# TensorE multiplies constant tiles while it waits: one kernel, 625 extra calls

## What is computed

```python
# first block, two layers, with 256 context tokens beside the 1024
h = rms_norm(x, gain) * (1 + scale) + shift
aq, ak, av, ag, bz, bg, nq, nk, nv, ng = split(h @ w_in)
a = softmax(rope(norm(aq)) @ [rope(norm(ak)), ak_ctx].T) @ [av, av_ctx]     # 8 heads, 2 key heads
b = pooled(bz) @ pool_w                                                     # four window widths
n = softmax([q @ k_neighbours.T + rpb, q @ k_ctx.T]) @ v                    # 4 heads, 8 x 16 window
x = x + gate * (concat(a * silu(ag), b * silu(bg), n * silu(ng)) @ w_out)
# second block
z = rmsnorm(x) @ w_in_2
y_fox = softmax(causal(q @ k.T * scale + c_i - c_j)) @ v                    # 8 heads, forgetting
y_rwkv = scan(r, w, k, v, a, b)             # state by chunks of 64 tokens, 16 chunks, 8 heads
x = x + (gates * (y_fox @ w_o_fox, y_rwkv @ w_o_rwkv)) @ w_out_2
x = x + (gelu(conv(rmsnorm(x) @ w_up)) * conv(...)) @ w_down
x = x + sigmoid(rmsnorm(x) @ w_ple_gate) * (p @ w_ple_up)
```

## Time and profile before

| | before |
|---|---|
| time, median of 3 runs | 4059.61 us (4057.88 to 4069.99) |
| the profiled execution: its time | 4062.47 us |
| its span, first to last instruction | 4060.7 us |
| TensorE busy with matmuls | 3622.6 us, 89% of the span |
| VectorE, GpSimd, ScalarE busy | 47%, 40%, 27% |
| mean granted clock of TensorE | 0.937 |

### The profile page before, as it was taken

One profiled execution on the slowest core, in us unless ns is written; L12 is line 12 of the kernel. 1 busy time (PEld: TensorE's weight loads), 2 busy tenths in 40 slices (PEclk: granted clock), 3 DMA queues, 4 the chain that ended last, 5 costly groups with the idle time before them and its releaser, 6 DMA issues. The chain is left out here.

```text
span 4060.7 us, 58584 instructions
## 1 busy us (share of the span) xinstructions
PE 3622.6 (89%) x25164; PEld 2712.6 (67%) x25164; DVE 1922.8 (47%) x1914; ACT 1098.3 (27%) x1544; POOL 1641.4 (40%) x897
## 2 busy tenths in 40 slices
PE   5999799879899798977999997787888899999988
PEld 4887333668678333766776776764467688888877
DVE  4442566552542565633549204434543562635542
ACT  3223344430223344411245212223410210101120
POOL 1332366442333366443347444402443344444433
PEclk9999799989899799988999999977889899999999
DMA  4012100044111100041211210020032111111111
GB/s 179 32 46 70 52 1 0 15 157 155 58 36 69 26 1 1 15 150 57 90 56 47 98 66 4 4 94 0 1 107 100 42 46 49 52 47 47 52 47 68
DMA packets 93736, 226.85 MB, mean 56 GB/s; under 512 B 28320, under 2 KB 37536, under 8 KB 92592
## 3 DMA queue, kind: packets, MB, share of 16 engines
q1 hardware_dynamic: 76096, 188.75, 13.5%
q10 hardware_dynamic: 17392, 34.48, 2.6%
HBM read 184.36 MB, written 38.83 MB: 55 GB/s over the span
## 5 line engine op out<-in xcount | busy, mean ns | idle before, releaser
L1719 PE MATMUL acc<-h_hi,weights_hi 128*128 128x512 f32 (+1 forms) x928 | 365.9, 394 | 24.6 <-DVE h_lo L1877 18.7
L988 DVE TENSOR_REDUCE part_max<-aux 128x2 f32<-128x856 f32 (+5 forms) x234 | 237.8, 1016 | 224.8 <-PE aux L836 154.8
L1721 PE MATMUL acc<-h_hi,weights_lo 128*128 128x512 f32 (+1 forms) x928 | 340.2, 367 | 0.0
L1720 PE MATMUL acc<-h_lo,weights_hi 128*128 128x512 f32 (+1 forms) x928 | 340.0, 366 | 0.0
L2396 PE MATMUL acc<-h_hi,weights_hi 128*128 128x512 f32 x672 | 274.2, 408 | 25.6 <-DVE h_lo L2674 15.7
L3297 PE MATMUL acc<-h_hi,weights_hi 128*128 128x512 f32 x704 | 276.0, 392 | 12.7 <-DVE h_lo L540 9.2
L3345 POOL TENSOR_TENSOR weights_hi<-weights,ones 128x1024 fp32r<-128x1024 f32 (+1 forms) x66 | 122.5, 1857 | 392.8 <-PE acc L3299 392.8
L3298 PE MATMUL acc<-h_lo,weights_hi 128*128 128x512 f32 x704 | 275.7, 392 | 0.0
L3299 PE MATMUL acc<-h_hi,weights_lo 128*128 128x512 f32 x704 | 275.4, 391 | 0.0
L1891 DVE RECIPROCAL arena<-arena 128x512 f32<-128x512 f32 (+1 forms) x48 | 141.7, 2953 | 263.3 <-ACT arena L1854 263.3
L2398 PE MATMUL acc<-h_hi,weights_lo 128*128 128x512 f32 x672 | 263.5, 392 | 0.0
(11 more groups left out here) (460 smaller groups left out, 8435.9 us busy)
## 6 DMA issues: line engine op xcount, KB each, us to landing
weights<-in_w_in SPq DMA_DIRECT2D x44, 512.0 KB, 3.3
weights<-in_w_up SPq DMA_DIRECT2D x43, 512.0 KB, 3.2
arena<-in_w_mod SPq DMA_DIRECT2D x6, 2048.0 KB, 9.6
weights<-in_w_out SPq DMA_DIRECT2D x21, 512.0 KB, 5.3
weights<-in_w_mod SPq DMA_DIRECT2D x4, 2048.0 KB, 26.4
mixer_gates<-arena SPq DMA_DIRECT2D x32, 256.0 KB, 2.0
x_between<-arena ACTq DMA_DIRECT2D x16, 512.0 KB, 3.8
weights<-in_w_gates SPq DMA_DIRECT2D x16, 512.0 KB, 3.3
```

Source lines behind the costliest of these rows:

```text
L988: nc.vector.tensor_reduce(part_max[:, b % 2, j, :, i:i + 1], max_tile(m)[:, :, 0:cw], AX_X, ALU.max, negate=True).then_inc(max_done, 1)
L1719: nc.tensor.matmul(out, w_hi[:, b, k, :], hi[:, k, cols], start=(k == 0), stop=False)
L1720: nc.tensor.matmul(out, w_hi[:, b, k, :], lo[:, k, cols], start=False, stop=False)
L1721: return nc.tensor.matmul(out, w_lo[:, b, k, :], hi[:, k, cols], start=False, stop=(k == KD - 1))
```

## The change

A function multiplies a constant 128 x 128 float32 tile (`cn["mean"]`, filled with 1/1024) by itself a given number of times, into 128 columns of a PSUM bank whose content nobody needs at that time. It signals nothing. It is called on TensorE ahead of waits. Where a wait guards the bank that is written, that wait is now made ahead of the call (`acc_free`, `kept`, `raw_ready` or `x_added`, and `row_copied` with `max_done` at a new pair). Nothing is removed. The counts, added up over the whole program, are about 625 calls.

```diff
+def keep_busy(pg, bank, times):
+    for _ in range(times):
+        pg.nc.tensor.matmul(bank[:, 0:P], pg.mean[:], pg.mean[:], start=True, stop=True)
@@ multiply
     if maker:
         maker.tensor(pe)
+        keep_busy(pg, acc[:, 0], 36)
         pe.wait_ge(w.parted, 4)
         pe.wait_ge(acc_free, 2)
         for k in range(nk):
+            if k == 2:
+                keep_busy(pg, pg.aux[:, 0], 12)
             maker.ready(pe, k)
...
         if b == 0:
+            keep_busy(pg, acc[:, 0], 16)
             pe.wait_ge(w.half_parted, 1)
...
         mm.then_inc(acc_ready, 1)
+    pe.wait_ge(acc_free, 3)
+    keep_busy(pg, acc[:, 0], 8)
@@ gemm_residual, ahead of the means (10 also in feed_forward)
                 if squares:
+                    if not beside:
+                        keep_busy(pg, pg.aux[:, 1], 10)
                     pe.wait_ge(sq_added, n - 1)
@@ pair_attention
+    n_ahead = len(order)
...
+                    if m == first_piece[b] and p and blocks[b - 1][2] < p:
+                        pe.wait_ge(row_copied, b)
+                        pe.wait_ge(max_done, m)
+                        keep_busy(pg, pg.aux[:, 0], 8 if own_keys else 4)
...
-                for kind, j, *i in order:
+                for at, (kind, j, *i) in enumerate(order):
                     if kind == "max":
+                        if at < n_ahead:
+                            keep_busy(pg, outs[1], first_idle if j == 0 else 2 if pieces[j][0] == 0 else 4)
                         maximum(j)
                     elif kind == "row":
+                        if at < n_ahead:
+                            keep_busy(pg, outs[1], 5)
                         row(j)
@@ transposes of values; neighbourhood attention
+                    if g == 2:
+                        keep_busy(pg, pg.acc[:, 0], 20)
...
+                    if i == 1:
+                        keep_busy(pg, banks[0], 8)
@@ project (44 in branches, 22 in feed_forward, 18 in gemm_gated_residual)
+                    keep_busy(pg, pg.acc[:, 0], 12 if opened else 36)
                     pe.wait_ge(parted, 2)
...
+                        pe.wait_ge(kept, kept_before(j, c))
                         if c == 0:
+                            if j == 2:
+                                keep_busy(pg, pg.acc[:, 0], 8)
                             pe.wait_ge(parted, j + 1)
-                        pe.wait_ge(kept, kept_before(j, c))
@@ rwkv_scan, outer(t, ci, s)
+                    if t >= n_tiles - 2 and s != 1 and (n, s) > (2 * (n_tiles - 2), 2):
+                        keep_busy(pg, region[0], 3)
```

More of the change, by code:

```diff
@@ L254, in part_weights, with multiply @@
             nc.gpsimd.tensor_tensor(w.lo[:, b], w.raw[:, b], full(w.hi[:, b]), ALU.subtract).then_inc(w.parted, 1)
-def multiply(nc, pe, w, rhs, acc, chunks, nk, acc_ready, acc_free, n, turns=1, maker=None, beside=None):
+def multiply(pg, pe, w, rhs, acc, chunks, nk, acc_ready, acc_free, n, turns=1, maker=None, beside=None):
+    nc = pg.nc
     def product(b, c0, cn, kr):
@@ L340, in _ @@
             def _(pe):
-                multiply(nc, pe, w, rhs, pg.acc, chunks, nk, acc_ready, acc_free, n)
+                multiply(pg, pe, w, rhs, pg.acc, chunks, nk, acc_ready, acc_free, n)
             @block.gpsimd
@@ L401, in _ @@
             def _(pe):
-                multiply(nc, pe, w, rhs, pg.acc, chunks, nk, acc_ready, acc_free, n, maker=maker, beside=beside)
+                multiply(pg, pe, w, rhs, pg.acc, chunks, nk, acc_ready, acc_free, n, maker=maker, beside=beside)
                 if squares:
+                    if not beside:
+                        keep_busy(pg, pg.aux[:, 1], 10)
                     pe.wait_ge(sq_added, n - 1)
@@ L683, in __init__, with pair_attention @@
         self.q, self.k, self.keys, self.maxima, self.blocks, self.v, self.bias = q, k, keys, maxima, blocks, v, bias
-def pair_attention(pg, cn, pairs, q_cols, totals, ring, beside=None, mask=None, parts=None):
+def pair_attention(pg, cn, pairs, q_cols, totals, ring, first_idle, beside=None, mask=None, parts=None):
     nc = pg.nc
@@ L2040, in query_pair @@
                         keys=(k_twice[:, kv, :], k_rest[:, kv, :]))
-        pair_attention(pg, cn, [query_pair(p) for p in range(4)], SEQ + q_ctx * P, [by_head(5), total[:]], 4, by_head(4))
+        pair_attention(pg, cn, [query_pair(p) for p in range(4)], SEQ + q_ctx * P, [by_head(5), total[:]], 4, 12 if last else 4, by_head(4))
     pg.end_section()
@@ L2115, in _ @@
                 maker.tensor(pe)
+                keep_busy(pg, pg.acc[:, 0], 18)
                 pe.wait_ge(p_parted, 2)
@@ L2205, in _ @@
             def _(pe):
-                multiply(nc, pe, w, y, pg.acc, MAIN, nk, acc_ready, acc_free, 2 * KD, turns=2)
+                multiply(pg, pe, w, y, pg.acc, MAIN, nk, acc_ready, acc_free, 2 * KD, turns=2)
             @block.gpsimd
@@ L2268, in forgetting_attention @@
         pair_attention(pg, cn, [forgetting_pair(p) for p in range(FOX_TILES)], SEQ,
-                       [k[:, 0, :].rearrange("p (h n) -> p h n", h=2), total[:]], 3, mask=causal[:, 1, :], parts=parts)
+                       [k[:, 0, :].rearrange("p (h n) -> p h n", h=2), total[:]], 3, 24, mask=causal[:, 1, :], parts=parts)
 def branches(pg, cn, x, names, cols, conv, ops, tail, end_decay, minus_c, drams):
@@ L2479, in norm @@
                         mm.then_inc(x_spread, 1)
+                    keep_busy(pg, pg.acc[:, 0], 44)
                     pe.wait_ge(parted, 2)
@@ L2496, in _ @@
                         j, c = divmod(i, 2)
+                        pe.wait_ge(kept, i - 3)
                         if c == 0:
+                            if j == 2:
+                                keep_busy(pg, pg.acc[:, 0], 8)
                             pe.wait_ge(parted, j + 1)
-                        pe.wait_ge(kept, i - 3)
                         for k in range(KD):
@@ L3301, in _ @@
                 maker.tensor(pe)
+                keep_busy(pg, pg.acc[:, 0], 22)
                 pe.wait_ge(w.parted, 4)
@@ L3311, in _ @@
                     kind, i, t = jobs[j]
-                    pe.wait_ge(w.parted, j + 3)
                     if jobs[j - 2][0] == "up":
@@ L3316, in _ @@
                         pe.wait_ge(x_added, downs.index(jobs[j - 2]) + 1)
+                    if j == 2:
+                        keep_busy(pg, pg.acc[:, 0], 8)
+                    pe.wait_ge(w.parted, j + 3)
                     rhs, nk = h if kind == "up" else g, depth(j)
@@ L3480, in build @@
         cn = {k: pg.sbuf(stack, k, [P, P]) for k in ("ident", "head_mean", "rot", "mean")}
+        pg.mean = cn["mean"]
         cn["eps"] = pg.sbuf(stack, "eps", [P, 1])
```

## The result

The changed kernel takes 4029.86 us (median; 4023.44 to 4032.30) against 4063.38 us (4057.88 to 4069.99) of the kernel before in the same session: a ratio of 0.9913, 95% interval 0.9897 to 0.9929. It is faster by 33.5 us. The forecast was 3989 us, a gain of 74 on the same median; the time lies in the stated range (3962 to 4040), but the gain is less than half of what was forecast, where the "half bridged" rival put it (4029).

A forecast was written before the change was run, and what follows sets the result against it. TensorE was taken to set the time nearly everywhere, with 328 us of its work at the low clock. Terms 24.4 + 21.7 + 10 + 3.3 + 4.3 + 4 + 6 + 4 - 5.5 = 72.2 us; forecast 3989 us, range 3962 to 4040.

The forecast's parts named there:

- half bridged: Rival: tiles end before the awaited work, the clock falls again; half the gains, 4029 us (4012 to 4047), chance 0.22.
- what is paid: Tiles on the path: 3.5 us in the two products without a gap, 2 us for late calls; 5.5 us in all.
- Price of a tile: One call is two matmuls, 0.22 us at full clock; about 625 calls take 137 us, or 269 at the low clock.
- slower rival: The clock stays at 0.50 under constant tiles, so calls outlast their cover: 40 us lost, 4102 us, chance 0.04.
- First maxima: Where TensorE and VectorE take turns in the attentions, matmul time is in line: 75% of 28.9 us, 21.7 us gained.
- New pair of heads: Attention blocks behind a change of pair: 0.42 us lost per low-clock us, 85% of 28.7 us regained, 24.4 us.
- Third weight tile: Six low-clock stretches behind waits of some 3 us, worth 11.1 us; 10 us taken as gain.
- Openings: Starts of products: 3.3 us gained at merging product and `w_out_2`, 4.3 of 15.3 us at six others with longer waits.
- Means, 4 us, transposes and neighbourhood, 6 us: Low clock in three places of means, 4 us gained; four stretches of transposes and neighbourhood attention, 6 us.
- Scan: Last four chunks, steps of 9.47 us at 0.50: 2.0 us gained over three steps, less about 2 us; 4 us.
- Products without a gap: Merging product and product with `w_out_2`: eight calls each added to the path without cover, 3.5 us paid.
- The rule against it: The skill's ramp penalty under 1% of span, as counter-estimate: at most 41 us gained, 4022 us or more.

The follow-up runs named there:

- thin tiles: The changed kernel with every constant tile multiplying one moving column instead of 128, calls and places unchanged: 4106.84 us, 1.012 of the kernel before.
- second execution: The changed kernel, unchanged, profiled once more: 4028.57 us, with 259.4 us of low clock.
- combined kernel: The changed kernel with 20 first tiles in both layers, twice the tiles between pairs, none in products without a gap: 4020.33 us, 0.9898 of the kernel before.

## Why the forecast was wrong

The direction was right, and that the clock rises with these tiles. The step that failed is **what is paid**: "2 x 8 x 0.22 = 3.5 us", and "I add 2 us for calls that end just late". It named the two products without a gap and treated nearly all other calls as covered by a wait. With thin tiles the price is 46 us instead of 5.5. In the changed kernel itself 18.8 us of it can be placed. From the work moved it comes out higher, at about 36 to 48 us, an estimate: 156.7 us times 0.42 to 0.5 (66 to 78), less the 30.2 gained. For half of the tiles the same sum gives 16 to 21 us, for twice the tiles (328.2 - 68.6 = 259.6 us moved, 109 to 130, less 13.3) 96 to 117 us for 311 us of tiles. The estimate takes every moved microsecond to be worth 0.42 or more, which is not shown; where VectorE sets the pace it was worth nothing.

The forecast's sum was 72.2 us and the span gave 30.2, which leaves 42.0. The placed price explains 13.3 of them (18.8 less 5.5). The new pairs gave 14.1 instead of 24.4, which explains 10.3 (3.2 by the second execution). The first maxima gave 14.3 us in the stretches that were priced and 2.6 in front of them (layer two and the second block) instead of 21.7, which explains 4.8. The other 13.6 us lie outside the attentions. The terms priced there, as read below, come out 3.9 us short together. The remaining 9.7 have no place; the stage "branches, scan" became 3.3 us longer, but it differs as much between two executions of the kernel before.

Point by point:

- **Price of a tile, count, rise of the clock.** Right: 1250 matmuls, means of 310 and 284 ns (forecast some 0.27 us). More of them ran at the low clock than forecast, 52.7 of 182.7 us, and the mean clock came to 0.966, not 0.98. The slower rival, that constant tiles don't lift the clock, is refuted as a general rule. Thin tiles, which do not lift it, cost +49 us, near the 40 worked out for this rival.
- **First maxima, 21.7 us.** Right in kind, too high in size. "All of a matmul's time is in line" held from the row of maxima on, the stretches of the earlier trace rows: a turn fell from 1.87 to 1.60 us, and the wait of 1.14 us was a cover. To the instructions that end these stretches, layer one went from 29.4 to 24.7 us (26.4 in the second execution), layer two from 11.4 to 7.6 and the second block from 36.5 to 30.8: 14.3 us in all (12.6). What the sum put at nothing is the run of twelve equal maxima in front of the row. VectorE set a pace of 0.95 us there, the cover was 0.22 us, and two calls take 0.71 us even at the full clock. Layer one lost 8.7 us there, 8.0 of them between the first maximum and the twelfth (11.87 to 19.86 us). The slower rival had priced just these calls, at 9 us for both layers. At the full clock they cost nothing (13.39 us in layer two, 13.60 before). The other 6.5 us are the calls ahead of the first maximum, behind a barrier.
- **New pair of heads, 24.4 us.** The price of 0.42 us per low us held: equal blocks take 29.56 us (1402.76 to 1432.32) instead of 32.71, and one block of layer one takes 32.80 us with 7.4 us of low clock in the first execution (626.84 to 659.64) and 29.71 without any in the second. But from the end of the first maxima to the last block copy the three attentions together went from 642.9 us to 628.8 in one execution and 621.7 in the other, gains of 14.1 and 21.2 us: the clock still fell in some blocks, and the 85% were too high. Doubling these tiles changed the time by nothing that could be measured.
- **Third weight tile, 10 us.** Right: the six stretches of the earlier trace rows, each with the wait ahead of it, went from 51.5 us to 41.1, and none has low clock in either execution of the changed kernel.
- **Openings.** Both short ones ran at 1.00 and gained 3.0 us (forecast 3.3). Of the six long ones five still have low clock behind the tiles; the sixth, where 2.10 us of the wait were left, has none. These six together were 3.6 us shorter in one execution and 1.7 longer in the other (forecast 4.3), so their gain can't be told from chance.
- **Means, 4 us, transposes and neighbourhood, 6 us.** Right: 3.6 and 5.4 us.
- **Scan, 4 us.** The size came out about right, by two courses rather than by one mean. From the start of the four chunks to the next mark of VectorE the two executions were 1.7 and 4.5 us shorter (3.6 and 6.4 in the table, whose mark in front moves by 1.8): 7.6 us a chunk at 1.00 (forecast near 7.5), 11 at 0.50. "Less about 2 us until the clock has risen" was too little: there were 20 us of low clock here and 34 in the combined kernel.
- **Products without a gap, 3.5 us.** Right: without their tiles the two products are 1.8 us shorter each in the combined kernel.
- **The rival that had the time** ("half bridged") had it for another reason. About half of the low-clock work did move, but that is also what the forecast's own gains amount to (77.7 of 164 us). Its number came out by luck: the tiles' price, which it does not name, took a large part.
- **The rule against it.** The Trainium skill (TensorE: Matmul & The Clock Gate, Part 1) puts the ramp penalty below 1% of a typical kernel's span. The bound drawn from it, at most 41 us and 4022 or more, was kept by the measured 33.5 us and 4029.86. But that is a net figure. The 142.7 us of work that moved between the thin and the real tiles are worth 60 us at 0.42, an estimate, or 1.5% of the span, with half of the low-clock work left; so the traces of this kernel disagree with the page.

What stays open: why a given block falls in one execution and not in the next (the same wait of 1.4 us was followed by 0.50 once and by 1.00 once), what the real tiles cost beyond the 18.8 us placed, and where the last 9.7 us of the forecast's gain went.

## What to carry to other kernels

Filling a wait with constant work is paid wherever another engine's turn is shorter than the filled turn. Give every place its own price before a filler is called covered: read the other engine's pace there (0.95 us in one run of maxima, 1.87 in the next), and ask whether the wait in the trace lies in front of a barrier or behind it (7.80 us in all, 2.05 behind it). One larger group ahead of a chain of dependent steps is worth a try: the same small groups within the chain cost at the low clock (11 us a chunk) and are cheap at the full one (7.6), and ten calls in front were followed by the full clock, though one execution only shows it. And price a filler by a run whose filler does nearly everything but the useful thing, as one column instead of 128 does.

## What the runs showed of the hardware

- FP32 matmuls of one column on 128 rows hold TensorE nearly as long as those of 128 (1.01 and 1.22 us for four at the low clock), yet leave the low-clock work almost where it was (314 against 328 us).
- TensorE was busy 23.38 of 23.89 us, and 33.10 of 34.13, with the clock at 0.50 throughout, on 64-row and 64 x 64 matmuls with constant tiles between them. The same chain begun at 1.00 stayed at 1.00 (chunks of 7.64 us).
- A wait of 1.38 us behind sixteen tile matmuls was followed by the full clock (1892.34 above). A wait of 1.41 us behind a block was followed by 0.50, and in the next execution of the same kernel a wait of 1.40 us at the same place by 1.00 (1403.82 above). The length of the wait alone does not decide it.
- A higher mean clock is no measure of success: 0.984 gave 4057 us, 0.975 gave 4008.
